# Four split weight buffers held until use, the low part written over the raw unit: a float32 transformer and state-space forward pass on one NeuronCore

## The chip, the cores and the metric

The kernel runs on one core of one Trainium2 chip. The metric is the device time of one execution in microseconds; less is better. The kernel before was timed three times: 1116.54, 1117.03 and 1117.87 us, the median is 1117.03 us.

## The reference, cut to what matters

Three blocks work one after the other on an activation of 256 tokens by 1024 channels, all in float32:

```python
x = x + concat(moba_attention(q, k, v), conformer_conv(u)) @ w_out        # first block
x = x + swiglu(rms_norm(x))
for i in range(2):                                                        # second block
    m = (fox_mixer, s5_mixer)[i](rmsnorm(x))       # attention with forgetting, then a state-space mixer
    x = x + rmsnorm(m)
    x = x + rmsnorm(swiglu(rmsnorm(x)))            # (silu(h @ w_gate) * (h @ w_up)) @ w_down
```

Nearly all arithmetic is in the products with weight matrices: 1024 by 2560 and 1024 by 1024 in the first block, 1024 by 4112, then 1024 by 1024 for the mixers' other projections, and three feed-forward parts of 1024 by 2816, twice, and 2816 by 1024. Every weight is read once.

## The kernel before, in words

**Weights as units.** Every weight matrix is cut into units of 1 MB, [128, 2048] float32. There are 145 of them in one fixed order (`plan_units`, from L112). The first block has u (4 units), q, k, v (2 each), o1 (4), f1 up (22) and f1 down (11), the second fox (16), o2 (4), f2 up (22), f2 down (11), s (4), glu (4), o3 (4), f3 up (22), f3 down (11). In the text s0 is the first unit of s, s3 its last, glu0 the one behind it.

**Splitting.** TensorE multiplies in a rounded float32 format. For full precision each operand is a high part plus a low part, and each product is three matmuls: high by high, high by low, low by high. A unit goes through three steps on three engines, each a function called by unit number n:

- `load_unit` (L325) on SyncE's queue (SP) reads unit n into raw buffer n % 4. It waits until the low part of unit n - 4 is done (`lo_done`), since that is the last reader of the raw buffer.
- `split_high` (L335) on ScalarE (ACT), L341: copies raw to `whi[n % 2]`, rounding. It waits for the landing, and, as there are two such buffers, until PE has used unit n - 2 (`used`).
- `split_low` (L343) on VectorE (DVE), L347: raw minus high into `wlo[n % 2]`. It waits for the high part.

PE then waits for `lo_done` of the unit and multiplies: `mm_features` (L350; 48 matmuls, L361 to L363), `mm_quarter` (L366; a half-k unit of 24 matmuls, L378 to L380) or `mm_k_pair` (L388; 24 matmuls, L404, L406, L408). The last matmul counts `used` up.

**What sets the order.** Every engine has its program written out by hand, and works through it in that order; a wait holds all that is behind it on the same engine. In a feed-forward stage the loads, splits and products run in a loop over pairs of a gate and an up unit (`pe_pair`, `act_pair`, `dve_pair`, from L527): ACT applies silu to the gate product, splits the next two units' high parts, rounds the product; DVE makes one low part, multiplies, makes the other. Elsewhere single splits stand between the stage's own work.

**Norms.** Between a stage's products and the next stage stand a post-norm (pm0 behind o2, pf0 behind f2 down, pm1 behind o3; `act_norms` L479, `dve_postnorm` L508) and a pre-norm: ACT squares the two row blocks, POOL makes the reciprocal root (`pool_rstd`, L493 and L496), DVE a scaled diagonal (`dve_scale`, L502), PE turns x with it (`pe_turn`, L434; six column tiles of block 0, six of block 1, then the other two), ACT and DVE split the result (L457, L468). Row block 0 of the last product is complete in the middle of its last unit, block 1 at the end. PE does dummy matmuls (`keep_warm`, L424) while it waits. Stages f1 and fp have a residual sum (L1756) and no post-norm.

**Around the change.** From 45 to 122 us DVE does q's and k's norm (from L1684) and two thirds of a 31-tap convolution (L1655, L1658) beside the splits. In the first attention and behind it the chain runs through DVE, POOL's powers and DVE's tables (L1740) to the convolution's high and low part (L1460, L1747), which o1's third unit needs. In f1 POOL computes tables for the state-space mixer, block by block, PE multiplies them (L653, L658) and ACT stores them in DRAM as R, O and K. At the end of f2 ACT issues the reads of R and O back into RTab and OTab, 4 MB each (L1552, L1553), just behind the last square of the norm. TTab, 4 MB in rows of 512 bytes from K, is read by SP (L1039) in eight DMAs once PE's `v_done` has come, and PE waits for it at L1347.

In stage s PE multiplies s0 to s3 into banks 0 to 3. ACT copies parts 0 and 2 of the result to uT (L1568), DVE parts 1 and 3 (L1877), each followed by the split of a unit: behind part i stands the split of unit s0 + 2 + i, for i up to 2, so that glu0 is split behind part 2 and ahead of part 3. Then PE turns uT (L1297), regroups it (L1306) and begins the state-space products (L1316, which count `v_done`). The scan and TTab follow, then PE's y products (L1347) and the glu units.

Of the kernel before, what the change touches and what calls it, by code (L numbers as in the profile page):

```python
# [24 lines left out]
P = 128  # L25
# [5 lines left out]
FT = DFF // P  # L31
# [16 lines left out]
UNIT = 2048  # L48
RAW = 4
RING = 2  # L50
# [8 lines left out]
class Program:  # L59
# [104 lines left out]
    def place(self):  # L164
# [19 lines left out]
        self.wraw = fixed("wraw", [P, RAW, UNIT], F32)  # L184
        self.whi = fixed("whi", [P, RING, UNIT], F32R)
        self.wlo = fixed("wlo", [P, RING, UNIT], F32R)
# [133 lines left out]
        s = self.sem  # L320
        self.landed = [s(f"raw_landed{i}") for i in range(RAW)]
# [4 lines left out]
    def load_unit(self, sp, n0, view, it=0):  # L326

        n = n0 + 4 * it
        if n0 >= RAW:
            sp.wait_ge(self.lo_done, n - RAW + 1)  # L330
        k = view.shape[1]
        dst = self.wraw[:, n0 % RAW, :].rearrange("p (k c) -> p k c", k=k)
        sp.dma_start(dst, view).then_inc(self.landed[n0 % RAW], 16)

    def split_high(self, act, n0, it=0):  # L335

        n = n0 + 4 * it
        act.wait_ge(self.landed[n0 % RAW], 16 * (n0 // RAW + 1) + 16 * it)
        if n0 >= RING:
            act.wait_ge(self.used, n - RING + 1)  # L340
        act.activation(self.whi[:, n0 % RING, :], self.wraw[:, n0 % RAW, :], ACT.Copy).then_inc(self.hi_done, 1)  # L341

    def split_low(self, dve, n0, it=0):  # L343

        n = n0 + 4 * it
        dve.wait_ge(self.hi_done, n + 1)
        dve.tensor_tensor(self.wlo[:, n0 % RING, :], self.wraw[:, n0 % RAW, :],  # L347
                          self.whi[:, n0 % RING, :].bitcast(F32), ALU.subtract).then_inc(self.lo_done, 1)
# [246 lines left out]
    def act_ffn(self, act, st, a, prep=False):  # L595
        n = self.first[st + ".up"]
        self.over_pairs(act, lambda dn, f0, it, fs: self.act_pair(act, st, n + dn, a, f0, it, fs),
                        (lambda b0, it, bs: self.act_prep(act, a, b0, it, bs)) if prep else None)
        n = self.first[st + ".down"]
        for i in range(FT // 2):  # L600
            if n + i + 2 < len(self.units) and i < FT // 2 - 1:
                self.split_high(act, n + i + 2)
            if prep and i % 2 == 1:
                self.act_prep(act, a, FP + i // 2)

    def dve_ffn(self, dve, st, a):
        n = self.first[st + ".up"]
        self.over_pairs(dve, lambda dn, f0, it, fs: self.dve_pair(dve, st, n + dn, a, f0, it, fs))
        n = self.first[st + ".down"]
        for i in range(FT // 2 - 1):  # L610
            if n + i + 2 < len(self.units):
                self.split_low(dve, n + i + 2)
# [385 lines left out]
def build(nc, io, out):  # L998
    with ExitStack() as ctx:
        m = Program(nc, ctx, io)  # L1000
# [7 lines left out]
        def _(sp):  # L1008
# [18 lines left out]
            n = 0  # L1027
# [3 lines left out]
            while n < len(m.units):  # L1031
                if n in starts:
                    n = ffn(*starts[n])
                else:
                    if n == first["o3"] + 1:

                        sp.wait_ge(*m.past("v_done", 4))
                        for t in range(T):
                            sp.dma_start(m.TTab[SC * t:SC * t + SC].rearrange("c (b i) w -> c b i w", i=GB),  # L1039
                                         m.Kd.rearrange("(i h c) b w -> h c b i w", i=GB, h=2)[  # L1040
                                             1, :, :, :, P - SC * t:2 * P - SC * t]).then_inc(sem("t_in"), 16)
                    m.load_unit(sp, n, m.units[n][0])
                    n += 1
# [328 lines left out]
        def _(act):  # L1372
# [96 lines left out]
            m.split_high(act, 14)  # L1469
            for r in range(RT):  # L1470
                m.act_squares(act, "f1", m.x[:, r, :], r, *m.past("f1_x_ready", r + 1))
            m.act_turn(act, "f1", (0, 1, 2, 3, 6, 7), gain=N2)
            m.split_high(act, 15)
# [14 lines left out]
            m.split_high(act, first["fox"] + 1)  # L1488
# [53 lines left out]
            for i in range(3):  # L1542
                m.split_high(act, n + 2 + i)
# [3 lines left out]
            m.split_high(act, n + 5)  # L1547
# [15 lines left out]
            m.split_high(act, n + 1)  # L1563
# [51 lines left out]
            for i in range(1, 4):  # L1615
                m.split_high(act, n + 1 + i)
            m.act_norms(act, "pm1", "f3", 4, "o3_first", n + 4)
            m.act_turn(act, "f3", (0, 1, 2, 3, 6, 7), gain=FFNPRE + 8)
            m.split_high(act, n + 5)
# [5 lines left out]
        def _(dve):  # L1625
# [124 lines left out]
            m.split_low(dve, 14)  # L1750

# [9 lines left out]
            m.split_low(dve, 15)  # L1761
# [8 lines left out]
            m.split_low(dve, n + 1)  # L1770
# [90 lines left out]
            for i in range(3):  # L1861
                m.split_low(dve, n + 2 + i)
# [3 lines left out]
            m.split_low(dve, n + 5)  # L1866
# [6 lines left out]
            m.split_low(dve, n + 1)  # L1873
# [85 lines left out]
            for i in range(1, 4):  # L1959
                m.split_low(dve, n + 1 + i)  # L1960
# [3 lines left out]
            m.split_low(dve, n + 5)  # L1964
# [52 lines left out]
```

## Time and profile before

| | |
|---|---|
| timed runs | 1116.54, 1117.03, 1117.87 us |
| profiled execution, first to last instruction | 1116.6 us, 16908 instructions |
| PE busy | 1032.9 us, 92% |
| DVE busy | 622.1 us, 56% |
| ACT busy | 469.8 us, 42% |
| POOL busy | 394.7 us, 35% |
| mean granted TensorE clock | 0.962 of full speed |
| read from HBM | 170.41 MB |

The span of the profiled execution runs from the first to the last instruction; the execution's own time is one of about the timed runs' size and is not listed apart. Times in the rows are microseconds; a row of the timeline begins with its start from the beginning of the span and its length. In a row of the timeline the bracket says how long the engine stood idle before it and what ended that. L numbers are lines of the kernel. In the DMA rows q1 is SP's queue and q10 ACT's, with packets, MB and the share of the 16 DMA engines' time; an issue's row ends with KB and the median time to landing. `PEclk` is the share of full speed that the throttle grants: 1.00 is 2.4 GHz, 0.50 is 1.2 GHz.

### The profile page before, as it was taken

How to read it: one execution, taken by the hardware profiler on the slowest of the kernel's cores; microseconds unless marked ns; L12 is line 12 of the kernel's file. 1: busy time of each engine (PE TensorE's matmuls, PEld its weight loads, DVE VectorE, ACT ScalarE, POOL GpSimd, SP SyncE). 2: the span in 40 equal slices, each digit the busy share in tenths (PEclk: the TensorE clock that was granted, in tenths of full speed). 3: DMA queues.
4: the chain of work that ended last, by engine and by line, in shares of the span. 5: the costliest groups of instructions: out<-in, count | busy, mean ns of one | idle time of the engine just before them, and what ended most of it. 6: DMA issues, size and time to landing. Idle time of an engine off the chain costs nothing.

```text
span 1116.6 us, 16908 instructions
## 1 busy us (share of the span) xinstructions
PE 1032.9 (92%) x6931; PEld 903.5 (81%) x6931; DVE 622.1 (56%) x572; ACT 469.8 (42%) x601; POOL 394.7 (35%) x394
## 2 busy tenths in 40 slices
PE   7998879999999998999999999999954999999997
PEld 6865658999998776778779999887913979999986
DVE  3699665555654445463556845445481555455544
ACT  4553234444343455455454344334301545443432
POOL 3569584778899604130059800001040010000000
PEclk9999589999999999999999999999986999999999
DMA  9532004667666755233245555557896254655550
GB/s 341 176 140 76 0 2 127 222 199 223 223 221 221 235 178 169 95 116 112 77 153 171 185 188 182 191 190 264 323 108 81 86 178 145 187 166 185 184 185 38
DMA packets 129890, 182.66 MB, mean 164 GB/s; under 512 B 4656, under 2 KB 103472, under 8 KB 129328
## 3 DMA queue, kind: packets, MB, share of 16 engines
q1 hardware_dynamic: 113872, 158.35, 46.7%
q10 hardware_dynamic: 15968, 23.61, 6.2%
q8 instruction: 36, 0.59, 0.3%
q14 instruction: 14, 0.11, 0.0%
HBM read 170.41 MB, written 11.53 MB: 163 GB/s over the span
## 4 chain that ended last, share of the span: by engine, by line
PE 73%; DVE 10%; POOL 5%; ACT 4%; issue 3%; DMA 3%; SPq 2%; POOLq 0%; ACTq 0%; DVEq 0%
PE ps L361 12%; PE ps L363 11%; PE ps L362 11%; PE ps L404 7%; PE ps L408 6%; PE ps L406 6%; PE ps L378 3%; PE ps L380 3%; PE ps L379 3%; DVE cacc L1658 3%; DVE wlo L347 2%; PE ps L434 2%; SPq L1039 2%; DMA TTab<-K_dram 2%; POOL otmp L629 2%
## 5 line engine op out<-in xcount | busy, mean ns | idle before, releaser
L347 DVE TENSOR_TENSOR wlo<-wraw,whi 128x2048 fp32r<-128x2048 f32 x145 | 351.2, 2423 | 328.0 <-ACT whi L341 328.0
L341 ACT ACTIVATE whi<-wraw 128x2048 fp32r<-128x2048 f32 x145 | 277.5, 1914 | 286.5 <-PE ps L408 131.7
L361 PE MATMUL ps<-actH,whi 128*128 128x256 f32 x1248 | 356.6, 286 | 3.4 <-DVE actL L1927 2.3
L362 PE MATMUL ps<-actL,whi 128*128 128x256 f32 x1248 | 353.9, 284 | 0.0
L363 PE MATMUL ps<-actH,wlo 128*128 128x256 f32 x1248 | 353.9, 284 | 0.0
L361 PEld LDWEIGHTS ps<-actH,whi 128*128 128x128 f32 x1248 | 240.5, 193 | 6.9 <-issue 3.9
L362 PEld LDWEIGHTS ps<-actL,whi 128*128 128x128 f32 x1248 | 240.5, 193 | 0.0
L363 PEld LDWEIGHTS ps<-actH,wlo 128*128 128x128 f32 x1248 | 240.4, 193 | 0.0
L493 POOL TENSOR_SCALAR rs<-ss 128x1 f32<-128x1 f32 (+2 forms) x27 | 9.1, 339 | 604.9 <-ACT nat L476 510.1
L404 PE MATMUL ps<-whi,gH 128*128 128x512 f32 x264 | 82.3, 393 | 0.0
L408 PE MATMUL ps<-whi,gL 128*128 128x512 f32 x264 | 82.1, 392 | 0.0
L406 PE MATMUL ps<-wlo,gH 128*128 128x512 f32 x264 | 81.9, 391 | 0.0
L378 PE MATMUL ps<-whi,actH 128*128 128x512 f32 x176 | 72.6, 412 | 3.8 <-DVE wlo L347 2.4
L380 PE MATMUL ps<-whi,actL 128*128 128x512 f32 x176 | 69.0, 392 | 0.0
L379 PE MATMUL ps<-wlo,actH 128*128 128x512 f32 x176 | 68.8, 391 | 0.0
L542 ACT ACTIVATE sg<-ps 128x512 f32<-128x512 f32 x33 | 19.8, 599 | 116.1 <-PE ps L363 116.1
L404 PEld LDWEIGHTS ps<-whi,gH 128*128 128x128 f32 x264 | 49.0, 188 | 11.7 <-issue 1.2
L408 PEld LDWEIGHTS ps<-whi,gL 128*128 128x128 f32 x264 | 49.6, 188 | 10.8
L406 PEld LDWEIGHTS ps<-wlo,gH 128*128 128x128 f32 x264 | 49.6, 188 | 10.6
L741 ACT ACTIVATE p<-ps,nmax 128x128 f32<-128x128 f32 (+1 forms) x48 | 19.8, 416 | 60.0 <-DVE nmax L753 59.9
L378 PEld LDWEIGHTS ps<-whi,actH 128*128 128x128 f32 x176 | 33.1, 188 | 12.6 <-DVE wlo L347 3.4
L558 DVE TENSOR_TENSOR prod<-sg,ps 128x512 f32<-128x512 f32 x33 | 22.7, 687 | 33.2 <-PE ps L363 33.2
(314 smaller groups left out, 1443.8 us busy)
## 6 DMA issues: line engine op xcount, KB each, us to landing
wraw<-in_ffn_w_gate SPq DMA_DIRECT2D x22, 1024.0 KB, 5.3
wraw<-in_ffn_w_up SPq DMA_DIRECT2D x22, 1024.0 KB, 5.3
wraw<-in_ffn_w_down SPq DMA_DIRECT2D x22, 1024.0 KB, 5.0
wraw<-in_fox_w_in SPq DMA_DIRECT2D x16, 1024.0 KB, 5.4
wraw<-in_w_gate SPq DMA_DIRECT2D x11, 1024.0 KB, 5.3
wraw<-in_w_up SPq DMA_DIRECT2D x11, 1024.0 KB, 5.6
wraw<-in_w_down SPq DMA_DIRECT2D x11, 1024.0 KB, 5.1
wraw<-in_w_in SPq DMA_DIRECT2D x10, 1024.0 KB, 7.9
```

Of the source, the lines that this page charges most:

```text
L341: act.activation(self.whi[:, n0 % RING, :], self.wraw[:, n0 % RAW, :], ACT.Copy).then_inc(self.hi_done, 1)
L347: dve.tensor_tensor(self.wlo[:, n0 % RING, :], self.wraw[:, n0 % RAW, :], self.whi[:, n0 % RING, :].bitcast(F32), ALU.subtract).then_inc(s ...
L361: pe.matmul(out, wh, self.actH[:, k, :], start=(i == 0), stop=False)
L362: pe.matmul(out, wh, self.actL[:, k, :], start=False, stop=False)
L363: last = pe.matmul(out, wl, self.actH[:, k, :], start=False, stop=(i == KT - 1))
L378: pe.matmul(out, xh, wh, start=(ka == 0), stop=False)
L379: pe.matmul(out, xh, wl, start=False, stop=False)
L380: last = pe.matmul(out, xl, wh, start=False, stop=(ka == KT - 1))
L404: pe.matmul(self.ps[:, base + 2 * r + c, :], h, w[0][c], start=st, stop=False)
L406: pe.matmul(self.ps[:, base + 2 * r + c, :], h, w[1][c], start=False, stop=False)
L408: last = pe.matmul(self.ps[:, base + 2 * r + c, :], l, w[0][c], start=False, stop=sp_)
L1658: i = dve.scalar_tensor_tensor(m.cacc[:, j, :], src, w, m.cacc[:, j, :], ALU.mult, ALU.add)
```

## The change

The buffers are four of each kind; together they take as many bytes as before (four raw, two high, two low before; four high, four raw and low in one after). The low part lies at the address of the raw unit. The load of unit n now waits until PE has used unit n - 4; the high part waits for the landing alone. In the programs of ACT and DVE the split of a stage's second unit moves from behind the norm's turn to ahead of the norm (f1, f2, s, f3), and that of fox's second unit from behind fp's turn to the end of f1. On SP the eight reads of TTab move from ahead of o3's second unit to ahead of its first.

```diff
-RAW = 4
-RING = 2
+RING = 4
...
-        self.wraw = fixed("wraw", [P, RAW, UNIT], F32)
+        self.wraw = fixed("wraw", [P, RING, UNIT], F32)
+        self.wlo = at("wlo", [P, RING, UNIT], F32R, self.where["wraw"])
         self.whi = fixed("whi", [P, RING, UNIT], F32R)
-        self.wlo = fixed("wlo", [P, RING, UNIT], F32R)
...
     def load_unit(self, sp, n0, view, it=0):
         n = n0 + 4 * it
-        if n0 >= RAW:
-            sp.wait_ge(self.lo_done, n - RAW + 1)
+        if n0 >= RING:
+            sp.wait_ge(self.used, n - RING + 1)
...
     def split_high(self, act, n0, it=0):
         n = n0 + 4 * it
-        act.wait_ge(self.landed[n0 % RAW], 16 * (n0 // RAW + 1) + 16 * it)
-        if n0 >= RING:
-            act.wait_ge(self.used, n - RING + 1)
-        act.activation(self.whi[:, n0 % RING, :], self.wraw[:, n0 % RAW, :], ACT.Copy).then_inc(self.hi_done, 1)
+        act.wait_ge(self.landed[n0 % RING], 16 * (n0 // RING + 1) + 16 * it)
+        act.activation(self.whi[:, n0 % RING, :], self.wraw[:, n0 % RING, :], ACT.Copy).then_inc(self.hi_done, 1)
...
     def act_ffn(self, act, st, a, prep=False):
         for i in range(FT // 2):
-            if n + i + 2 < len(self.units) and i < FT // 2 - 1:
+            if n + i + 2 < len(self.units):
                 self.split_high(act, n + i + 2)
...
     def dve_ffn(self, dve, st, a):
-        for i in range(FT // 2 - 1):
+        for i in range(FT // 2):
             if n + i + 2 < len(self.units):
                 self.split_low(dve, n + i + 2)
...
@@ build: SP @@
-                    if n == first["o3"] + 1:
+                    if n == first["o3"]:
                         sp.wait_ge(*m.past("v_done", 4))
...
@@ build: ACT, ahead of f1; DVE alike @@
             m.split_high(act, 14)
+            m.split_high(act, 15)
             for r in range(RT):
                 m.act_squares(act, "f1", m.x[:, r, :], r, *m.past("f1_x_ready", r + 1))
             m.act_turn(act, "f1", (0, 1, 2, 3, 6, 7), gain=N2)
-            m.split_high(act, 15)
...
@@ build: ACT, behind fp's turn; DVE alike @@
-            m.split_high(act, first["fox"] + 1)
...
@@ build: ACT, o2, and the same for o3; DVE alike @@
-            for i in range(3):
+            for i in range(4):
                 m.split_high(act, n + 2 + i)
             m.act_norms(act, "pm0", "f2", 4, "o2_first", n + 4)
             m.act_turn(act, "f2", (0, 1, 2, 3, 6, 7), gain=FFNPRE)
-            m.split_high(act, n + 5)
...
@@ build: ACT, stage s, behind the turn; DVE alike @@
-            m.split_high(act, n + 1)
```

## Rows read from the trace of the kernel before

**Rows 1.** The page, part 1 and part 5 (busy, mean ns, idle before, releaser).
```profile
PE 1032.9 (92%) x6931; PEld 903.5 (81%) x6931; DVE 622.1 (56%) x572; ACT 469.8 (42%) x601; POOL 394.7 (35%) x394
...
L347 DVE TENSOR_TENSOR wlo<-wraw,whi 128x2048 fp32r<-128x2048 f32 x145 | 351.2, 2423 | 328.0 <-ACT whi L341 328.0
```

**Rows 2.** The waits of PE (us in total, times, longest us).
```profile
PE ps L1347 <- DMA TTab<-K_dram: 20.0, 1, 20.0
PE ps L404 <- DVE actL L1747: 7.5, 1, 7.5
...
PE ps L378 <- DVE wlo L347: 2.4, 1, 2.4
...
PE ps L653 <- POOL ob L643: 2.1, 5, 0.4
...
PE ps L361 <- DVE wlo L347: 1.1, 2, 0.9
```

**Rows 3.** 940 to 1000 us: busy us (x) of PE, PEld, DVE, ACT, POOL; PEclk; DMA.
```profile
940.00:1000.00 60.00, 60.00 (x502) 60.00 (x502) 29.37 (x20) 26.52 (x22) 0.00 (x0) 1.00 0.60 188
```

**Rows 4.** The timeline, DVE in fo's gating.
```profile
542.89 1.28 DVE L1856 TENSOR_TENSOR nat<-nat,ga 128x512 f32<-128x512 f32 x2
```

**Rows 5.** The timeline at 58 to 62 us, DVE, ACT and POOL.
```profile
58.22 1.66 DVE L1658 SCALAR_TENSOR_TENSOR cacc<-hpad,vectors,cacc 128x256 f32<-128x256 f32 x4
61.26 2.29 DVE L347 TENSOR_TENSOR wlo<-wraw,whi 128x2048 fp32r<-128x2048 f32 x1 [1.38 <-ACT whi L341]
...
59.31 1.92 ACT L341 ACTIVATE whi<-wraw 128x2048 fp32r<-128x2048 f32 x1 [1.59 <-PE ps L380]
...
58.84 3.04 POOL L496 TENSOR_TENSOR rs<-rs,mhalf 128x16 f32<-128x16 f32 x1
```

**Rows 6.** Stage f1's norm: DVE's timeline, then the chain of waits.
```profile
179.76 2.44 DVE L1756 TENSOR_TENSOR x_res<-x_res,ps 128x1024 f32<-128x1024 f32 x2
...
184.34 0.34 DVE L502 TENSOR_SCALAR rdiag<-ident,rs 128x128 f32<-128x128 f32 x1 [0.86 <-POOL rs L496]
...
183.53 4.07 PE ps L434 x32
```

**Rows 7.** The timeline ahead of pm0, ACT and DVE.
```profile
558.10 1.92 ACT L341 ACTIVATE whi<-wraw 128x2048 fp32r<-128x2048 f32 x1 [3.52 <-PE ps L408]
...
567.70 1.22 DVE L515 TENSOR_TENSOR nat<-ps,postgain 128x1024 f32<-128x1024 f32 x1
```

**Rows 8.** DMA: all weight loads; issues in 749:750, 771:771.3, 780.5:782; queues in 784:792.
```profile
DMA to landing us min/median/max: 4.7/5.3/18.7
...
wraw<-in_s_w_in SPq DMA_DIRECT2D x1, 1024.0 KB, 6.7
...
OTab<-O_dram ACTq DMA_DIRECT2D x1, 4096.0 KB, 23.3
...
wraw<-in_s_w_glu SPq DMA_DIRECT2D x1, 1024.0 KB, 17.8
...
q10 hardware_dynamic: 98, 3.21, 93.3%
q1 hardware_dynamic: 96, 0.10, 3.6%
```

**Rows 9.** The timeline of stage s, ACT, DVE and PE.
```profile
781.63 0.60 ACT L1568 ACTIVATE nat<-ps 128x512 f32<-128x512 f32 x1 [3.16 <-PE ps L363]
...
798.90 0.69 DVE L1877 COPY nat<-ps 128x512 f32<-128x512 f32 x1 [1.04 <-PE ps L363]
...
799.74 1.94 PE L1297 MATMUL ps<-ident,nat 128*128 128x128 f32 x16 [0.88 <-DVE nat L1877]
```

**Rows 10.** Busy time and granted clock (PEclk) at 439 and at 800 us.
```profile
439.00:441.60 2.60, 0.05 (x1) 0.00 (x0) 0.47 (x1) 2.60 (x4) 1.45 (x2) 0.90 0.96 340
441.60:444.40 2.80, 2.77 (x13) 1.97 (x14) 1.82 (x1) 1.65 (x3) 0.00 (x0) 0.50 0.05 17
799.70:811.00 11.30, 9.48 (x176) 8.63 (x176) 5.43 (x8) 5.26 (x9) 0.00 (x0) 1.00 0.57 193
```

More of the change, by code:

```diff
@@ L320, in place @@
         s = self.sem
-        self.landed = [s(f"raw_landed{i}") for i in range(RAW)]
+        self.landed = [s(f"raw_landed{i}") for i in range(RING)]
         self.hi_done, self.lo_done, self.used = s("hi_done"), s("lo_done"), s("unit_used")
@@ L328, in load_unit @@
         n = n0 + 4 * it
-        if n0 >= RAW:
-            sp.wait_ge(self.lo_done, n - RAW + 1)
+        if n0 >= RING:
+            sp.wait_ge(self.used, n - RING + 1)
         k = view.shape[1]
-        dst = self.wraw[:, n0 % RAW, :].rearrange("p (k c) -> p k c", k=k)
-        sp.dma_start(dst, view).then_inc(self.landed[n0 % RAW], 16)
+        dst = self.wraw[:, n0 % RING, :].rearrange("p (k c) -> p k c", k=k)
+        sp.dma_start(dst, view).then_inc(self.landed[n0 % RING], 16)
     def split_high(self, act, n0, it=0):
         n = n0 + 4 * it
-        act.wait_ge(self.landed[n0 % RAW], 16 * (n0 // RAW + 1) + 16 * it)
-        if n0 >= RING:
-            act.wait_ge(self.used, n - RING + 1)
-        act.activation(self.whi[:, n0 % RING, :], self.wraw[:, n0 % RAW, :], ACT.Copy).then_inc(self.hi_done, 1)
+        act.wait_ge(self.landed[n0 % RING], 16 * (n0 // RING + 1) + 16 * it)
+        act.activation(self.whi[:, n0 % RING, :], self.wraw[:, n0 % RING, :], ACT.Copy).then_inc(self.hi_done, 1)
     def split_low(self, dve, n0, it=0):
@@ L346, in split_low @@
         dve.wait_ge(self.hi_done, n + 1)
-        dve.tensor_tensor(self.wlo[:, n0 % RING, :], self.wraw[:, n0 % RAW, :],
+        dve.tensor_tensor(self.wlo[:, n0 % RING, :], self.wraw[:, n0 % RING, :],
                           self.whi[:, n0 % RING, :].bitcast(F32), ALU.subtract).then_inc(self.lo_done, 1)
@@ L1614, in _ @@
             n = first["o3"]
-            for i in range(1, 4):
+            for i in range(1, 5):
                 m.split_high(act, n + 1 + i)
@@ L1618, in _ @@
             m.act_turn(act, "f3", (0, 1, 2, 3, 6, 7), gain=FFNPRE + 8)
-            m.split_high(act, n + 5)
             m.act_ffn(act, "f3", 4)
@@ L1750, in _ @@
             m.split_low(dve, 14)
+            m.split_low(dve, 15)
             def residual(st, base, first, used):
@@ L1760, in _ @@
             m.dve_turn(dve, "f1", (0, 1, 2, 3, 6, 7), gain=N2)
-            m.split_low(dve, 15)
             m.dve_ffn(dve, "f1", 4)
@@ L1769, in _ @@
             dve.tensor_tensor(m.wfL[:], m.wf[:], m.wfH[:].bitcast(F32), ALU.subtract).then_inc(sem("wf_split"), 1)
-            m.split_low(dve, n + 1)
             dve.wait_ge(*m.past("f_done", 1))
@@ L1860, in _ @@
             n = first["o2"]
-            for i in range(3):
+            for i in range(4):
                 m.split_low(dve, n + 2 + i)
@@ L1865, in _ @@
             m.dve_turn(dve, "f2", (0, 1, 2, 3, 6, 7), gain=FFNPRE)
-            m.split_low(dve, n + 5)
             m.dve_ffn(dve, "f2", 4)
@@ L1872, in _ @@
             m.dve_turn(dve, "s", (4, 5, 6, 7, 2, 3), gain=MIXPRE + 8)
-            m.split_low(dve, n + 1)
             for i in range(4):
@@ L1958, in _ @@
             n = first["o3"]
-            for i in range(1, 4):
+            for i in range(1, 5):
                 m.split_low(dve, n + 1 + i)
@@ L1963, in _ @@
             m.dve_turn(dve, "f3", (0, 1, 2, 3, 6, 7), gain=FFNPRE + 8)
-            m.split_low(dve, n + 5)
             m.dve_ffn(dve, "f3", 4)
```

## The prediction

> **What bounds the kernel now.** The page says first who is busy: TensorE (PE) for 92% of the span [rows 1]. Time of DVE or ACT saved is worth something only where PE stands still for it. PE's waits, read next, are few [rows 2]: 20.0 us for TTab's transfer, 7.5 us for the convolution's low part at L1747, and only 2.4 and 1.1 us for a split weight unit, whose low part is written at L347. The reader may set that against the 328.0 us that DVE idles before L347 for ACT's high part [rows 1]: almost all of that idle time costs nothing.
>
> Why, the steady stretch shows [rows 3]. From 940 to 1000 us PE is busy 60.00 of 60.00 us at full clock, with 502 matmuls: 0.12 us each, 5.7 us for a unit of 48. High part 1.92, low part 2.29, some 0.1 of hand-overs make 4.3 us, and PE works on the next unit meanwhile. The feed-forward stages are like this but for single moments of the second, and they gain nothing.
>
> **The change, part by part.** (a) *The low part is written over the raw unit.* Same 2048 elements, same two inputs. DVE writes over its own input elsewhere: L1856 does 512 elements in 0.64 us (1.28 for two) [rows 4], 1.25 ns an element, where L347 has 2.29 / 2048 = 1.12 without. I take 0 for the 145 low parts; bounds 0 both ways in the steady stretches, since 5.7 - 4.3 leaves 1.4 us of cover, and nothing there waits for a faster one.
>
> (b) *ACT's high part no longer waits for PE*, so what stood behind that wait moves forward. The 2.4 us at L378 stay, for DVE has its own taps in front of that low part. The one place where DVE idles on the chain is at 60 us [rows 5]: it is through with its taps at 59.88 (58.22 + 1.66) and idles 1.38 us to 61.26 for a high part that could start only at 59.31, when PE freed the buffer; q's norm stands right behind. With four buffers this high part runs ahead. POOL's rstd ends at 61.88 (58.84 + 3.04), the low part would end at 62.17 (59.88 + 2.29), and the norm starts then. Gain 1.38 us; up to 168 us DVE and POOL stay the chain (k's norm, the taps, the power tables), so it is kept. Bounds 0 (POOL's rstd held up by the low part beside it) and 1.6.
>
> (c) *Second unit split ahead of the norm, stage f1.* Its raw units land long before, so the low parts are done by some 176 us. DVE can then add row block 0 when PE has completed it, at 178.2 (half a unit, 2.8 us, ahead of its end), and not at 179.76 [rows 6]. But block 1 follows only at the unit's end, 181: its diagonal is ready at 184.68 (184.34 + 0.34), while PE turns block 0 until 185.06 (183.53 + 12 of 32 instructions in 4.07). Of 1.5 us only 0.4 gets through. Bounds 0 and 0.5.
>
> (d) *The same ahead of pm0, pf0 and pm1.* Here a wait takes the place of the one removed. The post-norm begins at 567.70, when the low part is through [rows 7]. After, the extra unit's load waits until PE has used the unit four before it. That was at 558.0 (ACT's high part at 558.10 waited for the same unit). The median landing of 5.3, 1.92, 2.29 and 0.1 give 567.6. Gain 0.1 to 0.2 at three places, 0.4 together. The landing is what is late next: with 6.7, as s1 has [rows 8], each place loses 1.2. Bounds +3.6 and -0.9.
>
> (e) *The load waits for "used", not for "low done".* This decides, I expect. Load n starts when unit n-4 is used; in steady stretches that leaves three units, 17 us, for 5.3 + 4.3: no cost. In stage s (units s0 to s3, then glu0) it does not. ACT issues two table reads of 4 MB at about 771, and the second lands 23.3 us later, at 794.4 [rows 8]. Before, glu0 went out ahead of them, and glu1, issued at 781 in their midst, took 17.8 us, to 798.6. After, glu0 waits for s0, and ACT's L1568, which waits for the same, starts at 781.63 [rows 9]: glu0 takes glu1's place. Between 784 and 792 SP's queue moved 96 packets, 0.10 MB, and ACT's 98 packets, 3.21 MB [rows 8]: one for one in packets, 1 KB against 33 KB. At 12 packets in a us glu0's 1024 get nowhere until the tables are in. I take its landing where glu1's was, 798.6.
>
> By the Trainium skill ("DMA: Bandwidth & Descriptors", Queues, rings and completion order) each engine changes between its queues packet by packet, typically with 9 to 17 descriptors in a packet. The turns agree with the 96 against 98; that a turn is worth 9 to 17 rows does not, here it was one row of 1 KB. By the page glu0 would land in time and the sum would be that of the first rival.
>
> Who stands behind glu0: in the code DVE has its low part *ahead* of the last copy of uT, L1877, which now starts at 798.90 as soon as PE is through [rows 9]. After: 798.6 + 1.92 + 2.29 = 802.8. PE's turns of L1297 (799.74) and the whole state-space stage behind them move by 3.9 us. Nothing absorbs that: v_done, TTab's eight issues on SP and the wait for them follow in sequence. Bounds 0 (landing in 5.3) and 4.7 (17.8 again, from 781.65). SP's order is changed too: TTab now goes out ahead of o3's first unit, but v_done, not that unit, holds it: 0. The later loads of glu and o3 keep 12 us or more: 0.
>
> (f) *The clock.* PE's idle before L1297 grows from 0.9 to 4.8 us. Idle of 2.6 us at 439 was followed by a granted clock of 0.50, 1.2 GHz, in the next 2.8 us, where 799.7 to 811 has 2.4 GHz [rows 10]. L1297 and L1306 take 1.94 us each there; I take 1.4 us more for them, half of 2.8. Bounds 0 and 7.6, all of PE's work up to v_done at 808.
>
> (g) The low parts shift against POOL's table work: PE waits 2.1 us for it in f1, and 1.1 us for low parts in f2 [rows 2]. That may go either way: 0, bounds -3.2 and +2.
>
> **The sum**: -1.4 - 0.4 - 0.4 + 3.9 + 1.4 = +3.1. On the profile's 1116.6 that is 1119.7. The three timed runs have a median 0.4 higher, so 1117.03 + 3 = 1120.0.
>
> **The rivals.** *A, glu0 arrives in time:* the two queues share by bytes. The 3.31 MB in 8 us of [rows 8] are 414 GB/s; at half of that 1 MB takes 5 us and lands by 789, before ACT asks for it, two units of 5.7 us after [rows 9]'s 781.6. Then only the gains are left, -2.3: 1114.7, not slower. Against it stand the 17.8 us of glu1 and the 96 packets; for it, that glu0 is now first in its queue. 0.17.
>
> *B, a second unit is caught.* s3 is now issued when f2's last unit ends. The table reads follow some 4 us behind (an estimate: the post-norm's blocks take 2.5 us each and begin 1 us before that end). s3's packets need about as long. If 200 are left, they take 16 us at 12 in a us, s3's high and low parts end behind the moment when PE wants them (781.6 + 2 x 5.7 = 793), and PE loses up to 3 us more; with the lower clock held longer 1123 to 1125. It decides once s3's landing is late by 1 us or more. 0.15.
>
> *C, slow landings ahead of the post-norms* (6.7), 2 more: 1122. This is also the case in which splitting ahead does not do what it says. 0.05. *D, the waits of (g) vanish:* 1117 to 1118. 0.08.
>
> **How the numbers follow.** My forecast has 0.55, A 0.17, B 0.15, C 0.05, D 0.08. The forecast's own range is 1118 to 1122.2 (stall 2.5 to 4.7, clock 0.4 to 2.5). For 8 in 10 the range goes from A, 1114.6, to the lower edge of B, 1123.4. A measurement can tell this kernel from no change from 0.2%, 2.2 us: below 1114.8 faster, above 1119.3 slower. Slower: 0.40 of the forecast, B and C, 0.60. Faster: half of A, 0.08. Same: the rest, 0.32.
>
> **What would show it.** In the profile after: the last copy of L1877 near 803 us with DVE waiting for L341 before it, and L341 for the DMA into wraw; a landing of 16 to 18 us for glu0; PE's wait before L1297 of 4 to 5 us, and a granted clock of 0.50 right behind it; TTab's wait still 20 us; L404's 7.5 us at L1747 unchanged, but 1.4 us earlier; steady stretches unchanged. I am wrong if glu0 lands within 12 us of its issue, if PE waits for L347 in the steady stretches, or if L347's typical 2.29 us changes.

## The result and the profile after: 0.7% slower, more than forecast

The kernel after takes 1124.69 us (median of 4, 1123.0 to 1126.62), the kernel before 1116.78 us beside it (median of 4). The ratio is 1.0072, with a 95% interval of 1.0051 to 1.0092. Forecast were 1120.0 us and a range of 1114.6 to 1123.4: the sign is right, the size is not, and the time lies outside the range.

A run's time is 1.86 us above its span (1123.0 against 1121.1 for the profiled execution of the kernel after). The profile that the prediction read has a span of 1116.6, so its execution took some 1118.5 us (an estimate from the two) and was one of the longer ones. A second profile of the same kernel, taken later, has 1114.0. The reader should therefore compare stage by stage, with two profiles of each kernel. This table gives the time from the first matmul of one stage to that of the next, worked out from the traces; the last column is the mended kernel of experiment 8.

| stretch (from its first matmul to the next one's) | before | before, again | after | after, again | mended |
|---|---|---|---|---|---|
| start to f1 up | 187.4 | 186.6 | 187.4 | 187.3 | 186.9 |
| f1 up | 140.8 | 140.7 | 137.5 | 137.5 | 137.6 |
| f1 down, to fox | 73.0 | 73.0 | 75.1 | 75.1 | 74.1 |
| fox, to o2 | 145.8 | 145.7 | 148.4 | 151.6 | 144.9 |
| o2, f2, to s | 228.7 | 228.8 | 228.2 | 228.4 | 228.2 |
| s0 to s3 | 17.4 | 17.4 | 17.4 | 17.4 | 17.4 |
| s3 to glu0 (S5's stage) | 72.7 | 71.4 | 76.6 | 77.0 | 70.4 |
| glu0 to the end | 251.0 | 250.5 | 250.5 | 250.4 | 250.7 |
| span | 1116.6 | 1114.0 | 1121.1 | 1124.8 | 1110.1 |

So there are two large losses, S5's stage (+3.9 to +5.6 us by the pair that is compared) and the middle of fox (+2.6 to +5.9), a gain in f1 up (-3.2) of which f1 down gives 2.1 back, 0.3 to 0.6 gained in o2 and f2, and little elsewhere.

**The page of the kernel after**, parts 1 and 5, answers to [rows 1]. Line numbers of the kernel after are 3 lower than before up to L1347, and 4 to 10 lower behind that; in kernels with a hold added they are 2 higher again.

```profile
PE 1035.7 (92%) x6931; PEld 906.9 (81%) x6931; DVE 622.9 (56%) x572; ACT 468.6 (42%) x601; POOL 391.9 (35%) x394
...
L344 DVE TENSOR_TENSOR wlo<-wraw,whi 128x2048 fp32r<-128x2048 f32 x145 | 354.5, 2451 | 306.3 <-ACT whi L338 306.2
```

PE's share is the same 92%, and the mean of a low part has grown by 28 ns; on the page alone nothing is wrong.

**The waits of PE**, which answer to [rows 2] (us in total, times, longest us).

```profile
PE ps L1344 <- DMA TTab<-K_dram: 18.6, 1, 18.6
...
PE ps L1294 <- DVE nat L1867: 4.6, 1, 4.6
...
PE ps L375 <- DVE wlo L344: 2.5, 2, 2.4
...
PE ps L772 <- POOL qa L1119: 1.5, 1, 1.5
...
PE ps L650 <- POOL ob L640: 0.9, 1, 0.9
```

Four changes: L1294 waits 4.6 us instead of 0.9, a wait of 1.5 us for POOL's `qa` is new, the five waits of 0.4 us for POOL's `ob` have become one of 0.9, and TTab's wait is 1.4 us shorter. The 2.4 us at L375 stayed, as forecast.

**TTab's reads end sooner.** PE does not come to TTab later: its wait begins 23.8 us after the issue of the first read, and 23.9 before. The reads take less time. From the issue of the last of the eight to its landing, in the chain that ended last, before and after:

```profile
830.73 21.45 DMA TTab<-K_dram
```

```profile
838.15 20.03 DMA TTab<-K_dram
```

Before, o3's second unit went out in the middle of that:

```profile
835.73 49.70 SPq L333 DMA_DIRECT2D wraw<-in_s_w_out  x3
```

This row joins three issues. The first, at 835.73, landed 18.7 us later, at 854.44, so it ran beside the end of TTab's reads. After, no load goes out behind TTab until PE has used glu's first unit, at 879. The two profiles of the kernel before have 21.4 us for the last read, the ten of kernels whose loads wait for `used`, experiment 4 among them, 19.8 to 20.6. From the first issue to the last landing it is 43.5 and 43.8 us against 42.0 to 43.0, a gain of about 1 us. No run moved that load alone.

**The stall in stage s**, the timeline of ACT and DVE, which answers to [rows 9].

```profile
782.71 0.60 ACT L1562 ACTIVATE nat<-ps 128x512 f32<-128x512 f32 x1 [4.97 <-PE ps L360]
...
799.54 1.91 ACT L338 ACTIVATE whi<-wraw 128x2048 fp32r<-128x2048 f32 x1 [4.72 <-DMA wraw<-in_s_w_glu]
...
801.49 2.29 DVE L344 TENSOR_TENSOR wlo<-wraw,whi 128x2048 fp32r<-128x2048 f32 x1 [10.13 <-ACT whi L338]
803.70 0.68 DVE L1867 COPY nat<-ps 128x512 f32<-128x512 f32 x1
```

ACT waits for the landing until 799.54, DVE's low part of glu0 follows, and the last copy of uT starts at 803.70, 15 us after DVE's copy of part 1 (788.47). The load had gone out at 782.7, when L1562 started (782.71). The DMA view, with the issue at 782.7 (KB, us to landing) and the queues from 785 to 793 (packets, MB, share):

```profile
wraw<-in_s_w_glu SPq DMA_DIRECT2D x1, 1024.0 KB, 16.8
```

```profile
q10 hardware_dynamic: 96, 3.15, 91.6%
q1 hardware_dynamic: 80, 0.08, 2.9%
```

It took 16.8 us, between the 5.3 of the other loads and the 17.8 of [rows 8], with 80 packets for SP and 96 for ACT, 0.08 against 3.15 MB. SP's first row comes at 786.7; from there to 793 the two queues move 80 packets each.

**Busy time and granted clock**, which answer to [rows 3, 10] (busy us (x) of PE, PEld, DVE, ACT, POOL; PEclk; DMA).

```profile
441.60:448.40 6.80, 4.74 (x22) 2.89 (x20) 1.48 (x1) 3.49 (x6) 2.52 (x1) 0.50 0.10 39
803.40:810.20 6.80, 5.67 (x27) 5.70 (x28) 2.36 (x4) 2.07 (x4) 0.00 (x0) 0.50 0.53 167
810.30:817.00 6.70, 5.71 (x148) 5.30 (x147) 2.91 (x5) 2.01 (x4) 0.00 (x0) 1.00 0.01 2
940.00:1000.00 60.00, 60.00 (x502) 60.00 (x501) 31.13 (x22) 24.30 (x21) 0.00 (x0) 1.00 0.60 186
```

Behind the stall PE works 6.8 us at 1.2 GHz. The steady stretch is what it was, 60.00 of 60.00 us.

**What was not forecast: fox.** First the kernel before, timeline of POOL and DVE behind the sums of the squares of q:

```profile
433.39 0.20 POOL L493 TENSOR_SCALAR rs<-ss 128x16 f32<-128x16 f32 x1 [4.64 <-DVE ss L1788]
...
433.68 2.91 POOL L496 TENSOR_TENSOR rs<-rs,mhalf 128x16 f32<-128x16 f32 x1
...
434.77 2.29 DVE L347 TENSOR_TENSOR wlo<-wraw,whi 128x2048 fp32r<-128x2048 f32 x1 [1.48 <-ACT whi L341]
...
437.75 2.71 POOL L1122 TENSOR_TENSOR qa<-qa,qkg 128x512 f32<-128x512 f32 x2 [1.16 <-DVE qa L1796]
```

Then the kernel after, at the same place:

```profile
433.24 2.27 DVE L344 TENSOR_TENSOR wlo<-wraw,whi 128x2048 fp32r<-128x2048 f32 x1
...
433.40 2.17 POOL L490 TENSOR_SCALAR rs<-ss 128x16 f32<-128x16 f32 x1 [3.69 <-DVE ss L1780]
...
439.37 4.75 POOL L1119 TENSOR_TENSOR qa<-qa,qkg 128x512 f32<-128x512 f32 x2 [0.81 <-DVE qa L1788]
...
440.63 2.45 DVE L344 TENSOR_TENSOR wlo<-wraw,whi 128x2048 fp32r<-128x2048 f32 x1 [0.74 <-ACT whi L338]
```

Before, DVE's low part started at 434.77, held back by ACT's wait for PE, and POOL's L493, the first step of the reciprocal root, had long read its sums (0.20 us). After, the high part is ready earlier, so the low part starts at 433.24, right behind the sum; L490 starts at 433.40 and takes 2.17 us, to 435.57, when the low part ends (435.51). The gain on q, two operations of L1119, meets the next low part (440.63) and takes 4.75 us instead of 2.71. PE waits 1.5 us for it, at a place where it had already stood for 2.58. At k's root, 12 us earlier, the same step also takes 2.17 us (421.00), and PE does not wait for it.

All five profiled kernels that have the freed splits in fox (after twice, experiments 3, 5 and 7) show both slow roots and a wait of 1.5 to 1.9 us. Their fox stage takes 148.4, 151.6, 150.2, 150.7 and 150.4 us, with the clock at 1.2 GHz for 6.8, 13.7 and three times 10.2 us in the same place.

### The profile page after: what moved, and what is told of

It reads as the page before. It is cut to its first block, busy times and chain, and to the rows that moved or that the text cites. A ratio compares the mean times of both kernels' runs of the same rounds, so it can differ in the third digit from the quotient of the medians.

```text
span 1121.1 us, 16765 instructions
## 1 busy us (share of the span) xinstructions
PE 1035.7 (92%) x6931; PEld 906.9 (81%) x6931; DVE 622.9 (56%) x572; ACT 468.6 (42%) x601; POOL 391.9 (35%) x394
## 4 chain that ended last, share of the span: by engine, by line
PE 73%; DVE 11%; POOL 5%; DMA 4%; ACT 3%; SPq 2%; issue 2%; ACTq 0%; POOLq 0%; DVEq 0%
PE ps L358 12%; PE ps L360 12%; PE ps L359 12%; PE ps L401 7%; PE ps L405 7%; PE ps L403 7%; DVE cacc L1651 3%; PE ps L375 2%; PE ps L377 2%; PE ps L376 2%; DVE wlo L344 2%; SPq L1036 2%; DMA TTab<-K_dram 2%; PE ps L694 2%; DMA wraw<-in_s_w_glu 1%
## 5 line engine op out<-in xcount | busy, mean ns | idle before, releaser
L344 DVE TENSOR_TENSOR wlo<-wraw,whi 128x2048 fp32r<-128x2048 f32 x145 | 354.5, 2451 | 306.3 <-ACT whi L338 306.2
L338 ACT ACTIVATE whi<-wraw 128x2048 fp32r<-128x2048 f32 x145 | 272.5, 1909 | 108.5 <-DMA wraw<-in_ffn_w_down 53.2
L490 POOL TENSOR_SCALAR rs<-ss 128x1 f32<-128x1 f32 (+2 forms) x27 | 9.2, 342 | 605.6 <-ACT nat L473 512.4
L375 PE MATMUL ps<-whi,actH 128*128 128x512 f32 x176 | 72.6, 413 | 4.0 <-DVE wlo L344 2.5
L544 ACT ACTIVATE gH<-prod 128x512 f32 (+1 forms) x33 | 20.9, 633 | 83.1 <-DVE prod L555 83.1
L626 POOL TENSOR_TENSOR rtb<-G,BB 128x512 f32 (+1 forms) x16 | 39.4, 2462 | 28.8 <-PE ps L655 24.9
```

What stands on the lines that cost most here:

```text
L375: pe.matmul(out, xh, wh, start=(ka == 0), stop=False)
L626: return pool.tensor_tensor(out, f[:, g, :].unsqueeze(3).to_broadcast([P, GB, n, SC]), w[:, g, :].unsqueeze(2).to_broadcast([P, GB, n, SC] ...
```

## The experiments

All ratios are to the kernel before on the same chip (three groups of runs; its medians there 1116.93, 1117.6 and 1116.9 us).

**1 and 2. Both kernels again.**

> The kernel before once more, for its span beside its time and for how far two profiles of one program differ. Theory 1 (everything lies inside the span): span 1116 to 1117, ratio 1.000, first product of glu at 865 to 867 us. Rival: the times of before lie some 2 us under those that a span gives after, because something outside the span has changed; then this run shows a time that lies within 0.5 us of its span, where the profiled run after had 1123.0 beside 1121.1.

> The kernel after once more. Theory: PE's wait before its turns of uT is 4 to 5 us again, glu0 lands 16 to 18 us after its issue, the wait for TTab is 18 to 20 us; the f1 stage is 3 us shorter than before and fox's heads 2 us longer. Rival (chance in the first profile): these differences change sign or vanish, and the span lies 3 us off 1121. Ratio expected 1.004 to 1.009.

Measured: 1116.28 us, ratio 0.9994 (0.9984 to 1.0005); and 1124.75 us, ratio 1.0062 (1.0048 to 1.0077). The result stands, and the rival for experiment 1 is out: the profiled execution took 1115.87 us with a span of 1114.0. Both spans missed what was expected, the one of before by 2 us (1114.0, not 1116 to 1117, with glu's first product at 863.5), the one of after by 3.7 (1124.8), though every wait named came as expected. The new profiles show how far one execution differs from another by the clock alone. The same work in attention, in the first profile of before and in the second (windows, PEclk ahead of the last two columns):

```profile
113.40:137.30 23.90, 21.74 (x71) 16.23 (x71) 16.39 (x33) 4.01 (x17) 14.12 (x31) 0.50 0.00 0
```

```profile
123.80:134.00 10.20, 10.20 (x33) 7.42 (x33) 3.96 (x11) 1.83 (x8) 4.57 (x14) 0.50 0.00 0
```

23.9 us at half clock against 10.2 (and 3.4 just ahead); o1 starts at 149.2 in the one and 145.0 in the other, of which 1.6 us are left at o1's third unit. In fox of the kernel after the lower clock lasted 6.8 us in the first profile and this long in the second, behind the same wait:

```profile
441.70:455.40 13.70, 11.38 (x39) 8.06 (x37) 1.92 (x3) 5.76 (x11) 2.34 (x1) 0.50 0.04 13
```

That is the 3.3 us by which the two profiles of the kernel after differ in fox.

**3. glu's first unit split late.**

```diff
-                if i < 3:
+                if i < 2:
                     m.split_high(act, n + 2 + i)
...
+            m.split_high(act, n + 4)
             m.split_high(act, n + 5)
```

(DVE alike; the split stands with the next one, behind the scan.)

> The kernel after, with glu0's split alone moved: its high part behind ACT's last copy of V and its low part behind the scan, each just ahead of glu1's. Nothing of stage s then stands behind glu0's landing. Theory 1 (the stall behind the table reads): PE's wait before its turns of uT falls from 4.6 to 0.9 us, the clock stays at 1.00 there, and the time falls by 4 to 5 us against the kernel after, to a ratio of 1.000 to 1.003 against before. Rival (the reads of the tables or TTab themselves are slowed by the later loads): the wait goes, but TTab lands later and the time stays within 1 us of after.

Measured: 1118.18 us, ratio 1.0012 (0.9999 to 1.0024). Waits of PE, and DVE's timeline:

```profile
PE ps L1294 <- DVE nat L1868: 0.9, 1, 0.9
```

```profile
798.60 0.69 DVE L1868 COPY nat<-ps 128x512 f32<-128x512 f32 x1 [8.63 <-PE ps L360]
```

The load still takes 16.9 us; the wait at L1294 is back at 0.9, and L1868 starts when PE is through. The S5 stage takes 71.1 us. The landing is harmless by itself; DVE's order makes it a stall.

**4. Only the load's wait and the place of TTab's reads changed, in the kernel before.**

```diff
-            sp.wait_ge(self.lo_done, n - RAW + 1)
+            sp.wait_ge(self.used, n - RAW + 1)
...
-                    if n == first["o3"] + 1:
+                    if n == first["o3"]:
```

> The kernel before with its buffers (four raw, two high, two low) and its splits where they were, but each load waits until PE has used the unit four before it, and TTab's reads stand ahead of o3's first unit, as after. Theory 1: this part alone brings the stall, glu0 landing near 799 us and PE waiting 4 to 5 us before its turns of uT, and nothing else: ratio 1.004 to 1.006, f1 and fox as before. Rival (the loss comes from the splits that run earlier): no more than 1 us of change, ratio 1.000.

Measured: 1122.1 us, ratio 1.0044 (1.0032 to 1.0057). Waits of PE:

```profile
PE ps L1297 <- DVE nat L1877: 4.9, 1, 4.9
```

The same stall without the new buffers: glu0 landed after 17.1 us, S5's stage takes 76.8 us, and f1 and fox are as before. The time is 5.8 us above the kernel before of experiment 1, 4.9 by the ratio. That is the stall less a gain: from the end of s3's products to TTab's first issue 15.2 us pass instead of 9.5, and TTab's reads are through in 42.1 us instead of 43.5 or 43.8.

**5. f1's high parts wait for PE again.**

```diff
+        if hold:
+            act.wait_ge(self.used, n - 1)
...
-        self.split_high(act, n0 + 3, it)
+        self.split_high(act, n0 + 3, it, hold=(st == "f1"))
```

> The kernel after, but in stage f1 (the pairs of gate and up units) the second of the two high parts waits again until PE has used the unit two before it. Theory 1: f1's gain of about 2.4 us came from this wait's removal alone, since the low parts no longer fell beside POOL's table work. Then the five waits of PE for POOL's table blocks (0.43 us each) are back, f2's first unit starts 2.0 to 2.5 us later against its neighbours than in the kernel after, and the time is 1126 to 1128 us, ratio 1.008 to 1.010. Theory 2: it came from the other order of the stage (the second unit split ahead of the norm, the pair's splits one place further on), which stays in this kernel. Then the waits stay away, and the time stays at 1124.7, ratio 1.007. In both the stall in stage s stays: 4 to 5 us of PE's wait ahead of the turn of uT.

Measured: 1126.93 us, ratio 1.0090 (1.0075 to 1.0106), and f1 up takes 140.7 us again. The interval just meets that of the kernel after, so the stage's time and the waits decide here. PE's wait, then DVE and POOL at the first block of tables:

```profile
PE ps L652 <- POOL ob L642: 2.1, 5, 0.4
```

```profile
198.35 2.48 DVE L346 TENSOR_TENSOR wlo<-wraw,whi 128x2048 fp32r<-128x2048 f32 x1 [1.32 <-ACT whi L340]
...
198.64 3.11 POOL L628 TENSOR_TENSOR otmp<-G,BB 128x512 f32 x1
...
205.79 3.39 POOL L642 TENSOR_TENSOR ob<-ob,otmp 128x576 f32<-128x576 f32 x1
```

The same place in the kernel before:

```profile
201.16 2.48 DVE L347 TENSOR_TENSOR wlo<-wraw,whi 128x2048 fp32r<-128x2048 f32 x1 [1.32 <-ACT whi L341]
...
200.43 1.07 POOL L629 TENSOR_TENSOR rtb<-G,BB 128x512 f32 x1 [6.58 <-PE ps L658]
201.46 3.11 POOL L629 TENSOR_TENSOR otmp<-G,BB 128x512 f32 x1
...
208.61 3.38 POOL L643 TENSOR_TENSOR ob<-ob,otmp 128x576 f32<-128x576 f32 x1
...
208.42 2.29 DVE L347 TENSOR_TENSOR wlo<-wraw,whi 128x2048 fp32r<-128x2048 f32 x1 [3.31 <-ACT whi L341]
```

and after:

```profile
199.80 2.29 DVE L344 TENSOR_TENSOR wlo<-wraw,whi 128x2048 fp32r<-128x2048 f32 x1
...
200.47 2.54 POOL L626 TENSOR_TENSOR rtb<-G,BB 128x512 f32 x1 [8.53 <-PE ps L655]
202.97 1.51 POOL L626 TENSOR_TENSOR otmp<-G,BB 128x512 f32 x1
...
208.18 1.44 POOL L640 TENSOR_TENSOR ob<-ob,otmp 128x576 f32<-128x576 f32 x1
...
208.45 3.31 DVE L344 TENSOR_TENSOR wlo<-wraw,whi 128x2048 fp32r<-128x2048 f32 x1 [4.90 <-ACT whi L338]
```

Theory 1 holds. The high part that need not wait brings the low part forward, by 1.36 us (199.80, not 201.16). It then lies beside `rtb` instead of `otmp`, and by the last operations of the block POOL is 0.4 us ahead. At the end of the block this decides who goes first: before, DVE's low part starts at 208.42 and POOL's L643 at 208.61, which takes 3.38 us; after, POOL's L640 starts at 208.18 and takes 1.44, and DVE's low part of 208.45 is the one that grows, to 3.31. The block ends at 209.62 instead of 211.99, ahead of PE's need, and DVE has the time to spare. The five waits of PE, one in every two pairs, are there with the hold (0.42 to 0.43 us each) and not without it. The wait of 0.9 us at 337 us, in f1 down, is the other way about: with the hold it is gone, and f1 down takes 74.4 us instead of 75.1.

**6. fox's high parts wait for PE again.**

```diff
-                    m.split_high(act, n + 2 * i + 2)
+                    m.split_high(act, n + 2 * i + 2, hold=True)
...
-                m.split_high(act, n + 2 * i + 3)
+                m.split_high(act, n + 2 * i + 3, hold=True)
```

> The kernel after, but in the units between fox's head sum and its end the high parts wait again until PE has used the unit two before. Theory 1: the loss of 2.2 us (4.7 with the lower clock behind it) in the middle of fox comes from a low part that, since ACT no longer waits, falls beside POOL's root of q's and k's norm (0.20 us before, 2.17 after) and its gain (2.71 before, 4.75 after). With the wait back POOL's two operations take 0.2 and 2.7 us, PE's wait for POOL of 1.5 us at 444 is gone, and the time is 1120 to 1122.5 us, ratio 1.003 to 1.005. Rival: POOL's loss comes from fox1's split that was moved ahead and shifts everything by 1 us, or from the level of the clock alone; then the wait for POOL stays and the time stays at 1124.7. The stall in stage s stays either way.

Measured: 1120.21 us, ratio 1.0024 (1.0012 to 1.0035). POOL and DVE, then the window behind it:

```profile
432.83 0.20 POOL L492 TENSOR_SCALAR rs<-ss 128x16 f32<-128x16 f32 x1 [4.67 <-DVE ss L1782]
...
437.19 2.70 POOL L1121 TENSOR_TENSOR qa<-qa,qkg 128x512 f32<-128x512 f32 x2 [1.17 <-DVE qa L1790]
...
434.22 2.29 DVE L346 TENSOR_TENSOR wlo<-wraw,whi 128x2048 fp32r<-128x2048 f32 x1 [1.47 <-ACT whi L340]
```

```profile
441.10:446.00 4.90, 3.68 (x28) 2.60 (x29) 1.76 (x1) 4.11 (x8) 0.00 (x0) 1.00 0.25 97
```

Theory 1: POOL's operations are back at 0.20 and 2.70 us, the new wait is gone, and fox takes 145.0 us. It takes 0.8 less than before, where both profiles show 3.4 us at 1.2 GHz behind PE's 2.58 us of standing; here PE stood 2.57 us and the clock stayed at 2.4 GHz. That is a difference between executions: experiment 10 has the same hold, 3.4 us at 1.2 GHz, and 145.9 us for fox. The rival, that the moved split of fox's second unit is the cause, is out by experiment 7, which puts it back: both roots still take 2.17 us there and PE waits 1.9 us for POOL.

**7. fox's second unit split behind fp's turn again.** 

```diff
-            if n + i + 2 < len(self.units):
+            if n + i + 2 < len(self.units) and (st != "f1" or i < FT // 2 - 1):
                 self.split_high(act, n + i + 2)
...
+            m.split_high(act, first["fox"] + 1)
             m.split_high(act, first["fox"] + 2)
```

(DVE alike.)

> The kernel after, but the split of fox's second unit stands behind fp's turn again. Theory 1: ahead of the norm it delays f1's residual sum by one low part's rest, 1.0 us; with it behind, the residual starts at PE's end, fox's first unit starts 1.0 us sooner against f1's end, and the time is 1123.2 to 1124, ratio 1.006. Rival: the residual is held by something else (the high part behind the O store's issue), then fox's second unit is late in its turn, or nothing changes: 1124.7, ratio 1.007. POOL's slow operations in the middle of fox and the stall in stage s stay.

Measured: 1123.67 us, ratio 1.0059 (1.0041 to 1.0076). In time that can't be told from no change, but f1 down is 1.1 us shorter (74.1), in this profile and in the three of mended kernels (experiments 8 to 10). DVE's timeline in the kernel after, then in this one, where f1 down began 0.1 us later:

```profile
390.35 2.29 DVE L344 TENSOR_TENSOR wlo<-wraw,whi 128x2048 fp32r<-128x2048 f32 x1 [6.64 <-ACT whi L338]
392.56 2.34 DVE L1750 TENSOR_TENSOR x_res<-x_res,ps 128x1024 f32<-128x1024 f32 x2
```

```profile
391.88 1.22 DVE L1751 TENSOR_TENSOR x_res<-x_res,ps 128x1024 f32<-128x1024 f32 x1 [1.53 <-PE ps L405]
```

In the kernel after the low part runs from 390.35 to 392.64 and the residual sum starts at 392.56, both blocks in one piece. Here block 0 is added at 389.13, in the middle of the last unit, and block 1 at 391.88, when PE is through.

**8 and 9. All three mended, twice** (the edits of 3, 6 and 7 together, with f1's gain kept).

> The kernel after with three places mended: glu's first unit split behind the last copy of uT, the wait of fox's high parts back between its head sum and its end, and the split of fox's second unit behind fp's turn. If the theory is whole (5 us in stage s, 2.2 to 5 in fox's middle, 1.0 ahead of fox, against gains of 2.4 in f1 that stay), the time is 1113.5 to 1115.5 us, ratio 0.997 to 0.999, faster than both kernels. Rival: the three losses overlap, or the gain of f1 is used up elsewhere (k's norm's gain was); then it is within 0.1% of the kernel before, 1116 to 1118.

> The kernel with the three places mended, once more: 1112.5 to 1114.5 us, ratio 0.996 to 0.998. If the first result was a favourable draw of the clock's low stretches, the ratio comes out above 0.998.

Measured: 1113.53 us, ratio 0.9967 (0.9955 to 0.998), and 1113.39 us, ratio 0.9972 (0.9958 to 0.9985). This version beats both kernels. The parts add up: the kernel after's ratio is 1.0067 (mean of its two). Alone, the edit of experiment 3 took 0.0050 off (1.0062 to 1.0012 beside each other), that of 6 took 0.0043 and that of 7 took 0.0008; that leaves 0.9966. Against the second profile of before, the table's gain is 2.1 us in f1 (net), 0.9 in fox, 0.6 in o2 and f2 and 1.0 in S5's stage. The 0.9 in fox is the clock of these executions and no gain of the program. The one in S5's stage goes with TTab's reads, 42.0 to 42.6 us from first issue to last landing in the mended kernels, where before has 43.5 and 43.8. PE's wait for k's norm, in experiment 8:

```profile
PE ps L774 <- DVE kn L1690: 3.9, 1, 3.9
```

**10. The high part at q's norm waits for PE again**, in the mended kernel.

```diff
-            m.split_high(act, 8)
+            m.split_high(act, 8, hold=True)
```

> The mended kernel, but the high part of v's first unit waits again until PE has used k's first unit, as in the kernel before. Theory 1: the 1.4 us gained at q's norm are eaten before o1's third unit, by PE's own wait in k's norm and by longer stretches of the clock at 1.2 GHz; then k's last norm is 1.3 to 1.5 us later against k's first unit, yet o1's third unit and the time stay within 0.5 us of the mended kernel: ratio 0.996 to 0.998, the same as beside it. Theory 2: the gain reaches the end, as I had forecast; then the time is 1.4 us longer than the mended kernel's, ratio higher by 0.0012.

Measured: 1113.64 us, ratio 0.9968 (0.9955 to 0.998), beside 0.9972 without the hold. PE's wait for k's norm:

```profile
PE ps L774 <- DVE kn L1690: 5.1, 1, 5.1
```

It is 1.2 us longer than the 3.9 without the hold. That wait also moves with the moment at which PE comes to it (3.6 us in the kernel before, 2.4 in experiment 6). A steadier measure is the time from PE's first matmul on k's first unit to its first on the normed k: 33.0 to 33.1 us in the four profiles in which this high part waits for PE (before twice, experiments 4 and 10), 31.6 in the eight in which it does not. So term (b)'s gain is real at its place; yet taking it away lost nothing that the times show, and the spans of this profile and of experiment 9's are both 1111.1. The interval is as wide as the 1.4 us in question, so this supports theory 1 rather than proves it.

## Why the prediction was right in part and wrong in size

Each term beside what the runs showed (us; below zero is a gain):

| term | forecast | measured |
|---|---|---|
| (b) q's norm | -1.4 | -1.5 at its place, -0.2 at o1's third unit, which is within the noise |
| (c) f1's second unit | -0.4 | -0.1 |
| (d) the same before three post-norms | -0.4 | -0.1 |
| (e) the wait ahead of the turn of uT | +3.9 | +3.7 to +4.1 |
| (f) the clock behind it | +1.4 | +1.5 to +2.6 |
| (g) tables in f1 up | 0 | -3.2 |
| (g) low parts in f2 up | 0 | -0.2 to -0.5 |
| f1 down: fox's second unit 1.1, a wait handed on 0.9 | none | +2.1 |
| POOL beside a low part in fox, with the clock | none | +2.6 to +5.9, and 4.8 by experiment 6's ratio |
| TTab's reads | 0 | -0.8 to -1.4 |

With 4.8 for fox and the middle of each span the measured column comes to between 7 and 8 us, as the times do: 1124.69 - 1116.78 = 7.9, and 7.5 by the mean ratio.

**The step that failed is (g)**: "That may go either way: 0, bounds -3.2 and +2." It put at nothing, without working it out, what the low parts do to POOL once ACT's wait no longer holds them, and it named only f1's tables and f2's low parts. The change moves *every* low part that this wait had held back, and POOL works beside DVE in fox and in the first block too. In f1 up the shift was worth -3.2, exactly the lower bound. In fox, which no term costs, it was worth +4.8 by experiment 6, and that is what carried the time out of the range. The bounds of (g) were also left out of the range, which ended at the lower edge of rival B. The same step hides in (b), which calls 60 us "the one place where DVE idles on the chain".

**That 1120.0 came as near as it did is luck.** Leaving fox aside, the gain in f1 up, the loss in f1 down, the gain of (b) that did not last and TTab's reads nearly cancel. Experiment 6, the kernel after without fox's loss, measured 1120.21 us: the forecast's figure, reached by other terms than the forecast's.

**The sign and the largest term were right.** (e): the wait at L1294 grew by 3.7 us (4.6 against 0.9), and each link named was there: the load caught behind the table reads, the low part of glu0 ahead of the last copy of uT. The first copy came 1.1 us later than in [rows 9] (782.71), and the landing took 16.8 us, not 17.8. (f): PEclk of 0.50 for 6.8 us behind it. From the end of s3's products to TTab's first issue, the stretch in which both fall, the six profiles with the stall take 5.2 to 6.6 us more than the 9.5 of before; (e) and (f) had 5.3. The table's (f) is what is left of this when the growth of the wait is taken off. "TTab's wait still 20 us" was wrong. The prediction put the new order on SP, and the later loads of glu and o3, at 0, yet o3's second unit no longer goes out beside TTab's last reads.

By the Trainium skill ("DMA: Bandwidth & Descriptors", Queues, rings and completion order) a queue's turn is a packet of typically 9 to 17 descriptors. Here a turn was again one row: in each of the five stretches of 1.25 us from 786.7 to 793, SP moved 16 packets of 1 KB and ACT 16 of 33 KB, one of each for every one of the 16 DMA engines. The prediction drew from the page that glu0 would land in time. That does not follow: if both queues move 9 to 17 rows in a turn, they are still even in rows, and 1 KB goes out for every 33. Rival A, which hung on the queues sharing by bytes, is refuted by every landing of glu0 in a kernel whose loads wait for `used`, 16.8 to 17.2 us in ten profiles.

**The prediction knew the effect of (g)**: for q's norm it set a bound of "0 (POOL's rstd held up by the low part beside it)". There it did not happen: L490 started at 58.64, ahead of the low part, whose rows are

```profile
59.98 2.28 DVE L344 TENSOR_TENSOR wlo<-wraw,whi 128x2048 fp32r<-128x2048 f32 x1
62.18 0.68 DVE L1677 TENSOR_TENSOR rtmp<-ps,rs 128x512 f32<-128x512 f32 x1
```

The norm starts at 62.18, where 62.17 was forecast. At the same pair of operations in fox the low part won the race by 0.16 us. The Trainium skill ("SBUF — State Buffer", SBUF: two separate sides) states the rule: the pair of ports that DVE and GpSimd share is a lock for the whole of an instruction, taken by whichever starts first of a POOL operation that reads SBUF and a DVE operation with two inputs in SBUF, and the other waits. L490 ending 0.06 us behind the low part agrees, and so do both ends of f1's block in experiment 5. POOL's L496 of 2.91 us, from 433.68, does not: the low part of 434.77 starts inside it, and neither is longer than elsewhere.

**(b), -1.4, was right at its place and did not reach the end.** PE's first matmul on the normed k came 1.5 us nearer to k's first unit (85.20 - 53.62 = 31.58, against 33.06). The prediction went on: "up to 168 us DVE and POOL stay the chain [...] so it is kept". From k's first unit to o1's third the four profiles without the gain take 113.5, 113.6 and twice 114.9 us, the eight with it 113.1 to 114.8. The means are 114.2 and 114.0, so about 0.2 of the 1.5 us is left, where profiles of the same kind differ by 1.4 to 1.7. What takes the rest stays open; PE's own wait and the stretches at 1.2 GHz, which differ from profile to profile there, are likely and not shown.

**The move of fox's second unit was costed in no term.** The parts name f1 and the three post-norms; this place has no post-norm, and it cost f1 down 1.1 us of its 2.1. Another 0.9 is POOL's wait that f1 up handed on (337 us). **(c) and (d)**: from the last product to the stage's first matmul it is 6.28 us instead of 6.41 in f1, and 8.71, 8.68 and 8.68 instead of 8.79, 8.70 and 8.70 in f2, s and f3. **(a)**, 0: right. A low part in place with no POOL operation beside it takes 2.29 us, as before; the mean of 2451 ns is the 57 of 145 that meet POOL (2.70 us each, where 56 took 2.63 before).

**Rival B** did not happen: s3 landed in 5.1 us and s0 to s3 take 17.4 us in all profiles. **C** did not either, by the gaps just named. **D**, that the waits of (g) vanish, did, and was priced at 2 us with a chance of 0.08; it was taken for a case of its own when it was a term that adds to the forecast.

**The base**: the sum was set on a profile read as 0.4 us below the median. With 1.86 us between span and time it was 1.5 above. The forecast of 1120.0 does not hang on it, since it adds the sum to the median, but the reading of stages from 1116.6 does.

## What to carry to other kernels

A wait that looks idle may be what keeps two engines apart: before a split is set free, list for each place which operation of POOL the earlier DVE operation with two inputs will meet, and which of the two starts first. A release point that is moved changes when each load goes out, so look for the one that falls into a long transfer, and for what stands behind its split on the same engine. Look behind the transfer as well: the moved load here also freed the end of TTab's reads. Free a buffer ring and set the order again, place by place: the change as it was made cost 0.7%, and with three splits put back or held it gained 0.3%.

## What was not expected of the hardware

- A POOL operation of 0.20 us takes 2.17 beside a low part that began 0.16 us sooner, and two that take 2.71 together take 4.75 when a low part falls between them; a POOL operation of 2.91 us on 128 by 16 elements and a low part that starts 1.09 us into it leave each other alone. Why these are spared stays open.
- After the same wait of PE in fox (2.58 us, with 1.5 to 1.9 us more in the kernels without the hold) the granted clock was 0.50 for 3.4 us in both profiles of before and in experiments 4 and 10, for 6.8 and 13.7 in those of after, for 10.2 in experiments 3, 5 and 7, and not at all in 6, 8 and 9. A single profile prices such a wait no better than to 3 us: the two of after differ by 3.3 us there.
- Two profiles of one program, before, differ by 2.6 us in span (1116.6 and 1114.0). The stretches at 1.2 GHz differ (37.9 and 22.4 us from k's first unit to o1's third), and some of PE's waits with them: L404's for the convolution is 7.5 us in the one and 10.1 in the other.
- A 1 MB load that went out behind TTab's last read landed after 18.7 us instead of 5.3, and that read after 21.4 instead of 19.8 to 20.6.
